# The S1 block of a weight pair added by DMA transfers from the Pool queue, in a one-core hybrid decoder step

## The chip, the cores and the metric

The kernel runs on one core of a Trainium2 chip. The metric is the device time of one execution in microseconds, as the median of several runs. Three runs of the kernel before gave 1041.46, 1042.13 and 1044.23 us.

## The reference, cut to what matters

One decoder layer is computed in float32 for 560 tokens (16 meta + 512 prompt + 32 sample): a SwiGLU feed-forward, a mixer (attention beside a short convolution), and a second SwiGLU feed-forward, each followed by a layer norm. The change touches only the two feed-forwards, and of them only the product with the gate and up weights:

```
D_MODEL = 1024; D_FF = 2816
def swiglu(x, wg, wu, wd):
    return (jax.nn.silu(x @ wg) * (x @ wu)) @ wd
x = layer_norm(DN_ALPHA * x + 0.5 * swiglu(x, wg_l[0], wu_l[0], wd_l[0]), g_l[0], b_l[0])
y, ks, vs, cs = token_mixer(x, attend, conv_prev, w_in_l, conv_w_l, w_out_l)
x = layer_norm(DN_ALPHA * x + y, g_l[1], b_l[1])
x = layer_norm(DN_ALPHA * x + 0.5 * swiglu(x, wg_l[1], wu_l[1], wd_l[1]), g_l[2], b_l[2])
```

## The kernel before, in words

**Units.** TensorE (PE) works through a list of weight units made by `plan_units`. A unit is one buffer of 128 x 1024 weights. Every unit is split in two before PE uses it: ScalarE (ACT) writes the rounded part (`w_hi` or `more_hi`), VectorE (DVE) subtracts it from the source to get the rest (`w_lo` or `more_lo`), and PE multiplies hi by hi, hi by lo and lo by hi. The split of a unit is made while PE works on units some places before it: `following(n)` names the unit that takes over the buffer of unit n, six places on.

**The pair stage.** In each feed-forward f (0 and 1) the first 256 columns of gate and up are done plainly ("gu"). The other 2560 columns are taken in ten pairs j = 0 to 9, each of 256 gate and 256 up columns. A pair is a 2 x 2 block product (blocks: upper and lower half of the contraction, gate and up; two halves of the tokens), done with seven block products instead of eight. Its four weight blocks are loaded by SP: a11 and a12 are the two halves of gate, a21 and a22 the two halves of up. The seven units s = 0 to 6 of a pair use a11, a12, S2, S1, the changed a11, the changed a12, and a22. Four block sums make them, all by DVE in `block_sum`, all 128 x 1024:

- sum 0: a11 <- a11 - a21 (in place)
- sum 1: a21 <- a21 + a22 (in place; this is the block S1, read by unit s = 3)
- sum 2: S2 <- a22 - a11
- sum 3: a12 <- a12 - S2 (in place)

Sum 0 must be over before sum 1, since it reads a21. Pairs 0 to 3 form chunk 0 and are followed by products with the down weights ("dn"); pairs 4 to 9 form chunk 1 and are followed by more of these.

**Order.** Every engine works through its own list in order; semaphores tie them together. While PE is in step s of pair j (`pair_step` of ACT and DVE), the two others do this, j+1 being the next pair:

| step s of pair j | ACT | DVE |
|---|---|---|
| 1 | hi of unit 0 of j+1; silu of the first half | c11 add; lo of unit 0 of j+1 |
| 2 | copy u2; hi of unit 1 | lo of unit 1; sums 0 and 1 |
| 3 | copy p5; hi of unit 2 (S2) | sums 2 and 3; lo of unit 2 |
| 4 | hi of unit 3 (S1) | c22 add; lo of unit 3 |
| 5 | silu of the second half; hi of unit 4; h1 hi | c12 add; lo of unit 4; h1 |
| 6 | h0 hi; hi of unit 5 | h0; lo of unit 5; h1 lo; h0 lo |
| 0 of j+1 | copy p1; hi of unit 6 | lo of unit 6 |

PE waits for copy p1 before step 2 of the same pair, for copy u2 before step 4, for copy p5 before step 5 and for the c22 add before step 6. For the first pair of a feed-forward (j = 0) the order is written out by hand in `gate_up_first`, where sum 1 comes after sum 3. For pair 4 the sums are made while PE is in the down products.

**Names and lines.** L1785 is the block sum, L1793 `block_lo`, L1364 `block_hi`, L1043 PE's pair product, L1442 copy p1, L1448 copy u2, L1452 copy p5, L1462 and L1469 the silus, L1472 and L1465 h1 hi and h0 hi, L1888 the c11 add, L1893 the c22 add, L1897 the c12 add, L714 SP's load of a block. Raw block buffers are called `w_raw` and `more_raw`. Pool (GpSimd) has no instruction in the pair stage.

Of the kernel before, what the change touches and what calls it, by code (L numbers as in the profile page):

```python
# [28 lines left out]
P = 128  # L29
# [33 lines left out]
QT = KT // 2  # L63
# [3 lines left out]
N_PAIRS = FT // 2 - 1  # L67
# [36 lines left out]
def pair_unit(f, j):  # L104
    return UNITS.index(("st", f, j, 0))
# [148 lines left out]
LOADS, RAW, LOAD_BEFORE, ARRIVED = plan_loads()  # L254
# [63 lines left out]
def build(nc, x_prompt, x_sample, cache_k, cache_v, state_conv, meta_tokens, rel_bias, w_in, conv_w,  # L318
# [4 lines left out]
    with ctx:  # L323
# [3 lines left out]
        def sem(name):  # L327
            return ctx.enter_context(nc.semaphore(name))
# [103 lines left out]
        weights_in = [sem(f"weights_in{i}") for i in range(RAWS)]  # L432
# [21 lines left out]
        combo_hi = sem("combo_hi")  # L454
        combo_ready = sem("combo_ready")
        blocks_summed = sem("blocks_summed")
        p1_copied = sem("p1_copied")
        u2_copied = sem("u2_copied")
        p5_copied = sem("p5_copied")
# [85 lines left out]
        def raw(key, k):  # L545

            r = RAW[key]
            return (w_raw[:, r, :] if r < SLOTS else more_raw[:, r - SLOTS, :]).rearrange("p (k n) -> p k n", k=k)

        def split_hi(n, k):  # L550
            at = SLOT[n]
            return (w_hi[:, at, :] if at < SLOTS else more_hi[:, at - SLOTS, :]).rearrange("p (k n) -> p k n", k=k)

        def split_lo(n, k):
            at = SLOT[n]
            return (w_lo[:, at, :] if at < SLOTS else more_lo[:, at - SLOTS, :]).rearrange("p (k n) -> p k n", k=k)

        def split_sum(n):

            at = SLOT[n]  # L560
            return (w_sum[:, at, :] if at < SLOTS else more_sum[:, at - SLOTS, :]).rearrange("p (k n) -> p k n", k=1)
# [781 lines left out]
        def _(act):  # L1343
# [8 lines left out]
            def block_hi(f, j, s):  # L1352

                n0 = pair_unit(f, j)
                n = n0 + s
                src = split_sum(n) if s == 2 else raw((n0, ("11", "12", None, "21", "11", "12", "22")[s]), 1)
                if s in (0, 1, 6):
                    key = (n0, ("11", "12", "22")[s // 1 if s < 2 else 2])
                    act.wait_ge(weights_in[RAW[key]], ARRIVED[key])
                else:  # L1360
                    act.wait_ge(blocks_summed, 4 * (N_PAIRS * f + j) + ({4: 1, 2: 2, 5: 3, 3: 4} if j == 0 else {4: 1, 3: 2, 2: 3, 5: 4})[s])
                if BEFORE[n] is not None:
                    act.wait_ge(steps_done, FREE[BEFORE[n]])
                nc.scalar.activation(split_hi(n, 1), src, ACT.Copy).then_inc(hi_ready, 1)  # L1364
# [357 lines left out]
            for k in range(WO_STEPS):  # L1722
                s = len(WI_STEPS) - AB + k
# [31 lines left out]
        def _(dve):  # L1755
# [9 lines left out]
            def block_sum(f, j, i):  # L1765

                n0, q = pair_unit(f, j), N_PAIRS * f + j
                a11, a12, a21, a22 = [raw((n0, b), 1) for b in ("11", "12", "21", "22")]
                s2 = split_sum(n0 + 2)
                if i == 0:  # L1770
                    dve.wait_ge(weights_in[RAW[n0, "21"]], ARRIVED[n0, "21"])
                    out, a, b, op = a11, a11, a21, ALU.subtract
                elif i == 1:
                    dve.wait_ge(weights_in[RAW[n0, "22"]], ARRIVED[n0, "22"])
                    out, a, b, op = a21, a21, a22, ALU.add
                elif i == 2:
                    dve.wait_ge(blocks_summed, 4 * q + 1)
                    dve.wait_ge(weights_in[RAW[n0, "22"]], ARRIVED[n0, "22"])
                    if BEFORE[n0 + 2] is not None:
                        dve.wait_ge(steps_done, FREE[BEFORE[n0 + 2]])  # L1780
                    out, a, b, op = s2, a22, a11, ALU.subtract
                else:
                    dve.wait_ge(blocks_summed, 4 * q + (2 if j == 0 else 3))
                    out, a, b, op = a12, a12, s2, ALU.subtract
                nc.vector.tensor_tensor(out, a, b, op).then_inc(blocks_summed, 1)  # L1785

# [8 lines left out]
            def next_lo(n):  # L1795

                if n is None:
                    return
                if UNITS[n][0] != "st":
                    weight_lo(n)  # L1800
                    return
                _, f, j, s = UNITS[n]
                if s == 2:
                    block_sum(f, j, 2)
                    block_sum(f, j, 3)
                block_lo(f, j, s)
                if s == 1:
                    block_sum(f, j, 0)
                if s == (2 if j == 0 else 1):
                    block_sum(f, j, 1)  # L1810

            def hidden(f, half, ab, first=False):

# [492 lines left out]
            for k in range(WO_STEPS):  # L2306
                s = len(WI_STEPS) - AB + k
# [39 lines left out]
        @block.gpsimd  # L2347
        def _(pool):
            def weight_lo(n):

                pool.wait_ge(hi_ready, n + 1)
                k = (KT - POOL_TILES) * P
                nc.gpsimd.tensor_tensor(split_lo(n, 1)[:, 0, k:], raw((n, ""), 1)[:, 0, k:],
                                        split_hi(n, 1)[:, 0, k:].bitcast(F32), ALU.subtract).then_inc(lo_pool, 1)

            def ln_sum_squares(L):
                s = ln_sum[:, L % 2, 0:ln_width(L)]
                for c in range(1, 4):
                    pool.wait_ge(squared, KT * L + c + 1)
                    if c >= 2:  # L2360
                        pool.wait_ge(sq_pool, 3 * L + c - 1)
                    nc.gpsimd.tensor_tensor(s, squares_of(L, 0) if c == 1 else s, squares_of(L, c), ALU.add
                                            ).then_inc(sq_pool, 1)

            def convolve(e):
                c, half = CONV_ORDER[e]
                pool.wait_ge(z_dve, step_count("h", c, half))
                if e >= 1:
                    pool.wait_ge(taps_added, 2 * e)
                if c >= 2:  # L2370
                    pool.wait_ge(z_dve, step_count("bg", c - 2, half))
                n = HALF if half == 0 else PROMPT - HALF
                for j in range(3):
                    w = C0 + CT * j + c
                    at = half * HALF + j
                    last = nc.gpsimd.tensor_scalar(taps[:, j, 0:n], u_p[:, c, at:at + n], coef[:, w:w + 1], None, ALU.mult)
                    if half:
                        last = nc.gpsimd.tensor_scalar(
                            taps[:, j, n:HALF].rearrange("p (b t) -> p b t", b=DEC_BATCH),
                            u_s[:, c, :, j:j + DEC_SEQ], coef[:, w:w + 1], None, ALU.mult)  # L2380
                last.then_inc(taps_done, 1)
                pool.wait_ge(taps_done, e + 1)
                nc.gpsimd.tensor_tensor(taps[:, 0, :], taps[:, 0, :], taps[:, 1, :], ALU.add).then_inc(taps_added, 1)
                pool.wait_ge(taps_added, 2 * e + 1)
                nc.gpsimd.tensor_tensor(conv[:, half, c % 2, :], taps[:, 0, :], taps[:, 2, :], ALU.add
                                        ).then_inc(taps_added, 1)

            for n in range(4):
                weight_lo(n)
            for L in range(2):  # L2390
                ln_sum_squares(L)
            for m in range(AB, len(WI_STEPS)):
                u, half = WI_STEPS[m]
                if WI_ORDER[u][0] == "h":
                    if m == WI_STEPS.index((WI_ORDER.index(("h", 0)), 0)):
                        pool.wait_ge(zero_done, 2)
                        pool.wait_ge(kct_copied, 1)
                    convolve(CONV_ORDER.index((WI_ORDER[u][1], half)))
            for k in range(WO_STEPS):
                if k == 8:  # L2400
                    ln_sum_squares(2)
            ln_sum_squares(3)
            pool.wait_ge(norm_rows_in, 32)
            for half in range(2):
                for i, (t, b) in enumerate(y_units(half, True)):

                    w, feats = Y_TILES[t][2], slice(512 * b, 512 * b + 512)
                    y = y_rows[0:w, t, feats]
                    pool.wait_ge(rows_normed, 2 * half + i + 1)
                    nc.gpsimd.tensor_tensor(y, y, g_row[0:w, feats], ALU.mult).then_inc(rows_pool, 1)  # L2410
                    pool.wait_ge(rows_pool, 2 * half + i + 1)
                    nc.gpsimd.tensor_tensor(y, y, b_row[0:w, feats], ALU.add).then_inc(y_pool, 1)
# [23 lines left out]
```

The launch sets the part of each SBUF partition kept for descriptors of Pool's DMAs:

```
nc = bacc.Bacc("TRN2", target_bir_lowering=False, num_devices=1, dynamic_dma_scratch_size=1024)
```

## Time and profile before

| | |
|---|---|
| median of 3 runs | 1042.13 us |
| the profiled execution, whole time | 1044.41 us |
| its span | 1042.6 us |
| mean granted TensorE clock | 0.982 |
| PE busy | 994.1 us (95%) |
| DVE busy | 690.8 us (66%) |
| ACT busy | 467.2 us (45%) |
| POOL busy | 69.6 us (7%) |
| DMA mean | 104 GB/s |

The profile is of one execution. Times in its views are microseconds from the start of the span. "Idle before <- releaser" says how long an engine stood still before an instruction and what released it. [...]

### The profile page before, as it was taken

What the parts mean: (1) busy time and instruction counts of PE and PEld (TensorE: products, weight loads), DVE (VectorE), ACT (ScalarE), POOL (GpSimd) and SP (SyncE); (2) the same over time, 40 slices, a digit from 0 to 9 for tenths busy, and PEclk for the clock granted to TensorE, in tenths of its full rate; (3) what the DMA queues carried; (4) which work ended last, traced back from release to release, by engine and by line L of the source; (5) the groups of instructions that cost most, each with busy time, mean ns of one, the idle gap of its engine ahead of it and who ended that gap; (6) DMA issues with size and microseconds to landing.
All of it is one profiled execution on the core that took longest, in us unless ns stands there. A gap on an engine that the chain in (4) does not pass through costs nothing. (4 is left out here: it accounts for less than half of the span.)

```text
span 1042.6 us, 18161 instructions
## 1 busy us (share of the span) xinstructions
PE 994.1 (95%) x7526; PEld 970.7 (93%) x7526; DVE 690.8 (66%) x990; ACT 467.2 (45%) x780; POOL 69.6 (7%) x80
## 2 busy tenths in 40 slices
PE   8979999999999999999999989679999999999994
PEld 7979999999999999999988988679999999999994
DVE  5887843577886468626666687787743587784457
ACT  4445531245445235545556456444521344553230
POOL 2000000000000000016142000000000000000004
PEclk9989999999999999999999999889999999999998
DMA  9463343133225333452113461033342222336402
GB/s 254 98 119 107 110 133 102 31 90 125 81 82 173 97 116 81 106 182 82 42 42 94 136 209 57 20 110 103 115 119 62 82 81 82 95 103 194 151 1 86
DMA packets 131594, 108.19 MB, mean 104 GB/s; under 512 B 13138, under 2 KB 129590, under 8 KB 131496
## 3 DMA queue, kind: packets, MB, share of 16 engines
q1 hardware_dynamic: 130368, 105.46, 34.1%
q10 hardware_dynamic: 1144, 1.57, 1.3%
q8 instruction: 60, 0.98, 0.4%
q14 instruction: 22, 0.18, 0.1%
HBM read 103.08 MB, written 4.95 MB: 104 GB/s over the span
## 5 line engine op out<-in xcount | busy, mean ns | idle before, releaser
L1056 PE MATMUL banks<-h_hi,w_hi 128*128 128x280 f32 (+1 forms) x480 | 139.1, 290 | 0.0
L1056 PE MATMUL banks<-h_hi,w_lo 128*128 128x280 f32 (+1 forms) x480 | 139.0, 289 | 0.0
L1056 PE MATMUL banks<-h_lo,w_hi 128*128 128x280 f32 (+1 forms) x480 | 138.8, 289 | 0.0
L877 PE MATMUL banks<-x_hi,w_hi 128*128 128x280 f32 (+1 forms) x416 | 126.3, 304 | 3.1 <-DVE x_lo L2127 0.9
L1043 PE MATMUL banks<-x_hi,w_hi 128*128 128x280 f32 (+1 forms) x400 | 118.5, 296 | 9.3 <-ACT ln_sq L1452 7.4
L877 PE MATMUL banks<-x_lo,w_hi 128*128 128x280 f32 (+1 forms) x416 | 120.8, 290 | 0.0
L877 PE MATMUL banks<-x_hi,w_lo 128*128 128x280 f32 (+1 forms) x416 | 120.7, 290 | 0.0
L1043 PE MATMUL banks<-x_hi,w_lo 128*128 128x280 f32 (+1 forms) x400 | 117.5, 294 | 0.0
L1043 PE MATMUL banks<-x_lo,w_hi 128*128 128x280 f32 (+1 forms) x400 | 117.3, 293 | 0.0
L1762 DVE TENSOR_TENSOR w_lo<-w_raw,w_hi 128x1024 fp32r<-128x1024 f32 (+1 forms) x66 | 77.9, 1182 | 56.6 <-ACT w_hi L1350 56.6
L1043 PE MATMUL banks<-t_hi,w_hi 128*128 128x280 f32 x336 | 99.7, 297 | 9.8 <-ACT silu_g L1442 8.8
L1043 PE MATMUL banks<-t_lo,w_hi 128*128 128x280 f32 x336 | 99.4, 296 | 0.0
L1043 PE MATMUL banks<-t_hi,w_lo 128*128 128x280 f32 x336 | 99.3, 295 | 0.0
L1350 ACT ACTIVATE w_hi<-w_raw 128x1024 fp32r<-128x1024 f32 x66 | 68.2, 1039 | 50.2 <-PE banks L1056 27.8
L1056 PEld LDWEIGHTS banks<-h_hi,w_hi 128*128 128x128 f32 x480 | 90.3, 188 | 0.0
L1056 PEld LDWEIGHTS banks<-h_hi,w_lo 128*128 128x128 f32 x480 | 90.3, 188 | 0.0
L1056 PEld LDWEIGHTS banks<-h_lo,w_hi 128*128 128x128 f32 x480 | 90.2, 188 | 0.0
L1043 PEld LDWEIGHTS banks<-x_hi,w_hi 128*128 128x128 f32 x400 | 77.0, 193 | 11.7 <-issue 11.7
L877 PEld LDWEIGHTS banks<-x_hi,w_hi 128*128 128x128 f32 x416 | 78.8, 189 | 7.1 <-DVE x_lo L1978 2.0
L1793 DVE TENSOR_TENSOR w_lo<-w_raw,w_hi 128x1024 fp32r<-128x1024 f32 x38 | 46.5, 1223 | 56.9 <-ACT w_hi L1364 56.9
L877 PEld LDWEIGHTS banks<-x_lo,w_hi 128*128 128x128 f32 x416 | 78.8, 189 | 1.5 <-issue 0.5
L877 PEld LDWEIGHTS banks<-x_hi,w_lo 128*128 128x128 f32 x416 | 78.8, 189 | 0.0
(236 smaller groups left out, 2660.0 us busy)
## 6 DMA issues: line engine op xcount, KB each, us to landing
w_raw<-in_ffn_w_down SPq DMA_DIRECT2D x30, 512.0 KB, 4.0
more_raw<-in_ffn_w_down SPq DMA_DIRECT2D x28, 512.0 KB, 3.6
w_raw<-in_ffn_w_gate SPq DMA_DIRECT2D x24, 512.0 KB, 4.0
w_raw<-in_ffn_w_up SPq DMA_DIRECT2D x24, 512.0 KB, 4.7
more_raw<-in_ffn_w_gate SPq DMA_DIRECT2D x20, 512.0 KB, 4.1
more_raw<-in_ffn_w_up SPq DMA_DIRECT2D x20, 512.0 KB, 5.5
w_raw<-in_w_in SPq DMA_DIRECT2D x14, 512.0 KB, 4.6
w_raw<-in_w_out SPq DMA_DIRECT2D x32, 128.0 KB, 3.0
```

Of the source, the lines that this page charges most:

```text
L877: mm = nc.tensor.matmul(out[:, 0:n], w[:, t, :], x(k), start=(k == ends[0] and w is hi and x is rhs_hi), stop=(k == ends[1] and w is lo))
L1043: mm = nc.tensor.matmul(out[:, ab, c0:HALF], w[:, k, ab * P:(ab + 1) * P], b(t, k), start=(new and k == 0 and w is hi and t[0] is x_hi), s ...
L1056: mm = nc.tensor.matmul(out, w[:, k - k0, c * P:(c + 1) * P], h[:, k, cols(half, f)], start=(k == 0 and w is hi and h is h_hi), stop=(ku = ...
L1350: nc.scalar.activation(split_hi(n, 1)[:, 0, 0:k], raw((n, ""), 1)[:, 0, 0:k], ACT.Copy).then_inc(hi_ready, 1)
L1762: nc.vector.tensor_tensor(split_lo(n, 1)[:, 0, 0:k], raw((n, ""), 1)[:, 0, 0:k], split_hi(n, 1)[:, 0, 0:k].bitcast(F32), ALU.subtract).the ...
L1793: nc.vector.tensor_tensor(split_lo(n, 1), src, split_hi(n, 1).bitcast(F32), ALU.subtract).then_inc(lo_ready, 1)
```

## The change

The block sum 1 (S1) leaves DVE. Pool issues, for each pair, two DMA transfers of 256 KB that read the a22 block again from the weights in HBM and add it into the a21 block in SBUF. Pool waits for sum 0 first. ACT's hi of unit 3 waits for the two transfers by a new semaphore `s1_summed`; the counts of `blocks_summed` go from four to three in a pair. Pool's list gets the ten pairs of feed-forward 0 after its first four weight splits and the ten of feed-forward 1 after the sums of squares of layer-norm half L = 3. The loads of a21 and a22 by SP stay, as do sums 0, 2 and 3.

```diff
@@ block_hi (ACT)
                     act.wait_ge(weights_in[RAW[key]], ARRIVED[key])
+                elif s == 3:
+                    act.wait_ge(s1_summed, 32 * (N_PAIRS * f + j + 1))
                 else:
-                    act.wait_ge(blocks_summed, 4 * (N_PAIRS * f + j) + ({4: 1, 2: 2, 5: 3, 3: 4} if j == 0 else {4: 1, 3: 2, 2: 3, 5: 4})[s])
+                    act.wait_ge(blocks_summed, 3 * (N_PAIRS * f + j) + {4: 1, 2: 2, 5: 3}[s])
@@ block_sum (DVE)
-                elif i == 1:
-                    dve.wait_ge(weights_in[RAW[n0, "22"]], ARRIVED[n0, "22"])
-                    out, a, b, op = a21, a21, a22, ALU.add
                 elif i == 2:
-                    dve.wait_ge(blocks_summed, 4 * q + 1)
+                    dve.wait_ge(blocks_summed, 3 * q + 1)
                 else:
-                    dve.wait_ge(blocks_summed, 4 * q + (2 if j == 0 else 3))
+                    dve.wait_ge(blocks_summed, 3 * q + 2)
@@ next_lo (DVE)
                 if s == 1:
                     block_sum(f, j, 0)
-                if s == (2 if j == 0 else 1):
-                    block_sum(f, j, 1)
@@ Pool
+            def second_row_sum(f, j):
+
+                n0, q = pair_unit(f, j), N_PAIRS * f + j
+                pool.wait_ge(blocks_summed, 3 * q + 1)
+                w = w_up[0, f].rearrange("(k p) n -> p k n", p=P)
+                for k in range(0, QT, 2):
+                    nc.gpsimd.dma_start(raw((n0, "21"), QT)[:, k:k + 2, :],
+                                        w[:, QT + k:QT + k + 2, (2 + 2 * j) * P:(4 + 2 * j) * P],
+                                        accum_op=ALU.add).then_inc(s1_summed, 16)
+
             for n in range(4):
                 weight_lo(n)
+            for j in range(N_PAIRS):
+                second_row_sum(0, j)
@@ Pool, after the loop over WO_STEPS
             ln_sum_squares(3)
+            for j in range(N_PAIRS):
+                second_row_sum(1, j)
```

## Rows read from the trace of the kernel before

**Rows 1.** Part 1 of the page: busy time, share, instructions.

```profile
PE 994.1 (95%) x7526; PEld 970.7 (93%) x7526; DVE 690.8 (66%) x990; ACT 467.2 (45%) x780; POOL 69.6 (7%) x80
```

**Rows 2.** Windows: stretch, busy of each engine, clock, DMA share, GB/s.

```profile
877.00:899.00 22.00, 21.81 (x172) 21.62 (x171) 17.56 (x19) 11.20 (x15) 0.00 (x0) 1.00 0.31 96
61.00:66.00 5.00, 0.50 (x3) 0.50 (x3) 4.45 (x5) 2.14 (x3) 0.00 (x0) 0.79 0.61 105
68.00:70.00 2.00, 2.00 (x10) 2.00 (x10) 1.97 (x3) 0.44 (x1) 0.00 (x0) 0.50 0.73 148
660.00:669.00 9.00, 0.24 (x3) 0.09 (x1) 8.97 (x10) 3.40 (x6) 0.00 (x0) 0.76 0.00 0
681.00:684.00 3.00, 0.14 (x2) 0.00 (x0) 2.48 (x4) 2.11 (x3) 0.00 (x0) 1.00 1.09 372
686.00:688.00 2.00, 2.00 (x11) 2.00 (x9) 2.00 (x2) 0.00 (x0) 0.00 (x0) 0.50 0.00 0
```

**Rows 3.** Waits of PE: line, releaser, us in total, times, longest.

```profile
PE banks L1043 <- DVE ln_sq L1893: 2.5, 14, 0.2
```

**Rows 4.** Timeline of DVE, one pair: start, us, instruction, [idle before <-releaser].

```profile
707.82 2.35 DVE L1785 TENSOR_TENSOR more_raw<-more_raw 128x1024 f32<-128x1024 f32 x2
...
713.62 0.73 DVE L1893 TENSOR_TENSOR ln_sq<-ln_sq,banks 128x560 f32<-128x560 f32 x1
714.26 1.22 DVE L1793 TENSOR_TENSOR w_lo<-more_raw,w_hi 128x1024 fp32r<-128x1024 f32 x1
...
721.97 1.23 DVE L1793 TENSOR_TENSOR more_lo<-more_raw,more_hi 128x1024 fp32r<-128x1024 f32 x1 [1.66 <-ACT more_hi L1364]
...
725.52 0.70 DVE L1888 TENSOR_TENSOR silu_g<-silu_g,banks 128x528 f32<-128x528 f32 x1
...
728.45 1.23 DVE L1793 TENSOR_TENSOR w_lo<-w_raw,w_hi 128x1024 fp32r<-128x1024 f32 x1 [1.09 <-ACT w_hi L1364]
729.59 2.35 DVE L1785 TENSOR_TENSOR w_raw<-w_raw 128x1024 f32<-128x1024 f32 x2
```

**Rows 5.** Timeline of ACT, the same pair.

```profile
712.30 1.04 ACT L1364 ACTIVATE w_hi<-more_raw 128x1024 fp32r<-128x1024 f32 x1
716.16 0.67 ACT L1462 ACTIVATE ln_sum<-ln_sum 128x560 f32<-128x560 f32 x1 [2.82 <-DVE ln_sum L1897]
...
721.84 0.62 ACT L1442 ACTIVATE silu_g<-banks 128x560 f32<-128x560 f32 x1
...
726.25 0.65 ACT L1469 ACTIVATE silu_g<-silu_g 128x528 f32<-128x528 f32 x1 [1.40 <-DVE silu_g L1888]
726.83 0.64 ACT L1448 ACTIVATE ln_sum<-banks 128x560 f32<-128x560 f32 x1
727.37 1.05 ACT L1364 ACTIVATE w_hi<-w_raw 128x1024 fp32r<-128x1024 f32 x1
```

**Rows 6.** Timeline of PE, three places in feed-forward 1.

```profile
668.94 0.57 PE L1043 MATMUL banks<-t_hi,w_hi 128*128 128x280 f32 x1 [8.76 <-ACT silu_g L1442]
...
691.21 0.36 PE L1043 MATMUL banks<-x_hi,more_hi 128*128 128x264 f32 x1 [2.29 <-DVE w_lo L1793]
...
723.53 0.29 PE L1043 MATMUL banks<-t_hi,w_hi 128*128 128x280 f32 x1
```

**Rows 7.** Timelines of DVE and ACT: pair 0 (S1), pair 4 (sum 0, next ACT work).

```profile
663.80 1.22 DVE L1785 TENSOR_TENSOR more_raw<-more_raw 128x1024 f32<-128x1024 f32 x1
...
805.21 1.22 DVE L1785 TENSOR_TENSOR w_raw<-w_raw 128x1024 f32<-128x1024 f32 x1
...
818.01 1.06 ACT L1364 ACTIVATE w_hi<-w_raw 128x1024 fp32r<-128x1024 f32 x1 [4.97 <-PE banks L1056]
```

**Rows 8.** DMA issues: median us from issue to landing; block loads of 650 to 760.

```profile
w_raw<-in_w_in SPq DMA_DIRECT2D x14, 512.0 KB, 4.6
w_raw<-in_w_out SPq DMA_DIRECT2D x16, 256.0 KB, 3.4
w_raw<-in_w_in SPq DMA_DIRECT2D x8, 256.0 KB, 3.9
...
DMA to landing us min/median/max: 3.8/4.3/6.3
```

More of the change, by code:

```diff
@@ L456, in build @@
         blocks_summed = sem("blocks_summed")
+        s1_summed = sem("s1_summed")
         p1_copied = sem("p1_copied")
```

## The prediction

> **What bounds the kernel now.** I read part 1 of the page first: TensorE is busy 95% of the span, DVE 66%, Pool 7% [rows 1]. So a microsecond taken from DVE counts only where PE waits for it. The windows say where that is. In the middle of the pair stage PE is busy 21.81 of 22 us with DVE at 17.56 [rows 2]. PE stands still in two places, the entry into the pair stage of each feed-forward: 4.5 of 5 us from 61 to 66, 8.8 of 9 us from 660 to 669, and nearly all of 681 to 684, with DVE busy through most of each. PE's own waits end on ACT's copy p1 (8.76 us, at 668.94) and on a DVE weight split (2.29 us, at 691.21) [rows 6]; inside the stage the c22 add costs 14 waits of at most 0.2 us, 2.5 us in all [rows 3].
>
> The timelines of one pair say more than the busy shares. DVE and ACT form a closed loop of hand-overs with next to no slack. From lo of unit 3 (714.26) to the next sum 0 (729.59) every stop of one engine is ended by the other, and none by PE: DVE c12 add, ACT silu (waited 2.82 us for DVE), hi and lo of unit 4, h1, h1 hi, h0 hi, hi of unit 5, lo of unit 5 (waited 1.66 for ACT), h1 lo, h0 lo, lo of unit 6, c11 add (725.52), silu, copy u2 (726.83), hi of unit 1, lo of unit 1 (waited 1.09), sum 0 [rows 4, 5]. That is 729.59 - 714.26 = 15.33 us of a period of 729.59 - 707.82 = 21.77 us. The rest is the DVE queue: sums 0 to 3, lo of unit 2, c22 add, lo of unit 3. DVE's average of 80% in this stage hides that the loop is as long as PE's own work.
>
> **Part 1: what the removal gives.** 20 sums leave DVE. Two in a row take 2.35 us and one alone 1.22 [rows 4, 7], so each holds the queue for 1.13 us, 22.6 us in all. It lies beside PE work except where the loop or the heads end a wait of PE: (a) pair 0, where S1 at 663.80 stands in the chain that ends in copy p1: 1.13 us in each feed-forward [rows 6, 7]; (b) the c22 add of the next pair, before PE's step 6 at 691.21: another 1.13 us each; (c) the 2.5 us of waits for the c22 add [rows 3]. Sum, if nothing replaces it: 4 x 1.13 + 2.5 = 7 us. No more, because PE's work is then the next bound.
>
> **Part 2: what the new wait adds.** The wait stands in ACT's in-order list before hi of unit 3. Behind it on ACT stand the silu of the second half, hi of unit 4, h1 hi, h0 hi, hi of unit 5 and copy p1; on DVE, lo of unit 3 waits for that hi, and the c12 add and everything after it stand behind lo. So the transfer enters the loop. Let L be the time from the end of sum 0 to the start of hi of unit 3 by way of Pool's wait, two issues, the landing and the semaphore. Nothing else is in Pool's queue there (busy 0.00 in the stage [rows 2]), and SP's queue is not passed.
>
> - From hi to lo: 728.45 - 727.37 = 1.08 us [rows 4, 5], then 15.33 us, then 1.18 us of sum 0 (half of the pair's 2.35). New loop: 17.59 + L. Old period: 21.77. Each further pair costs L - 4.18.
> - PE notices at step 2, by copy p1. It ended at 721.84 + 0.62 = 722.46, 8.20 us after lo of unit 3, so 9.28 us after hi starts. PE's step 2 began at 723.53, which is 14.53 us after sum 0's end (709.00) [rows 4 to 6]. The first late block of a chunk costs PE L - 5.25.
> - Chunk 1 has five such blocks (pairs 5 to 9): 4(L - 4.18) + (L - 5.25) = 5L - 21.97. Chunk 0 has three (pairs 1 to 3) and begins 1.13 us early by (a): 3L - 14.74. Both feed-forwards: 16L - 73.4.
> - Pairs 0 and 4 are covered. Sum 0 of pair 4 is over at 806.4 and ACT's next work stands at 818.01 [rows 7]; less 2 us for hi and its queue, L up to 9.6 is free there. In pair 0 it is about 8 us.
>
> **What L is.** No row has a Pool DMA or an adding one. The nearest: a 256 KB block of SP lands 3.4 to 3.9 us after its issue, a 512 KB block 4.6 in the median, and the loads of this stage 3.8 to 6.3 [rows 8]. From below: both transfers fly as one plain load would, L = 3.8, where the change gains. From above: two in a row, each as long as the slowest load, 12.6. I take two in a row, since the code cuts the block in two where SP's loads are whole: 2 x 3.65, plus 2 x 0.6 for reading the destination as well (the step from 256 to 512 KB, 4.6 - 3.9 = 0.7, nearly). That is 8.5 with no charge for Pool's own work in making the transfers, for which there is no row. HBM is no limit: 20 x 512 KB more beside 93 to 96 GB/s.
>
> [...]
>
> With L = 8.5: 16 x 8.5 - 73.4 = 63 us.
>
> **The clock.** A PE that stood 2.9 us (681 to 684) runs at 0.50 from 686 to 688; one that stood 4.5 us is at 0.50 from 68 to 70 [rows 2]. These spells last some 3.3 and 5 us and cost half of that, 1.6 and 2.5. Here PE would stop 4.3 us in each pair: I take 2.0. In the loop copy u2 waits for PE's step 2: without PE it would come 12.57 + 1.08 = 13.65 us after hi of unit 3, and step 2 now ends 9.4 + 3.1 + 2.0 = 14.5 us after it. So 0.9 us in each of 12 pairs, and 2.0 in full in the last pair of each of 4 chunks: 11 + 8 = 19 us.
>
> **Sum.** 63 + 19 = 82 us on the profiled execution's 1044.4, which is 1126. That execution is 2.3 us above the median of the runs: on the median 1124. I say 1125.
>
> **Rivals.**
> - A, the other side: the transfers land within 4.2 us, so the loop gets shorter and the 7 us of part 1 come through: 1037 on the profiled execution, 1035 on the median. It decides at L = 4.18, and at 73.4 / 16 = 4.6 the account is even. For it: a plain 512 KB block lands in 3.8 at best [rows 8]. Against: Pool has to be woken, there are two transfers, and each also reads its destination. Chance 0.07. [...]
> - B, overlap: the second is issued while the first moves. L = 5.5 to 7, 16L - 73.4 = 15 to 39, clock up to 10: 1060 to 1091. Chance 0.22.
> - C, Pool starved: making the transfers is slow, or slowed by DVE's block sums that run just then (sums 2 and 3, lo, c22 add, 4.6 us without a gap [rows 4]). L = 12 to 13, 119 to 135 us and a clock loss of 35: about 1200. [...] Chance 0.13.
> - D: L about 4.6, no change. Chance 0.03.
>
> **The numbers.** Forecast 0.55 (L from 7 to 11). The range goes from L = 5.6 (16 us, no clock loss: 1060) to L = 11.5 (111 us and 27 of clock: 1182). A measurement of this kernel tells 0.3%, 3 us, from no change. Slower 0.90, same 0.03, faster 0.07.
>
> **What would show it.** In the profile after: ACT's wait before hi of unit 3, ended by a DMA, 16 times, and L read from it; sum 0 to sum 0 spaced by 17.6 + L, some 26 to 27 us; PE idle at step 2 (first instruction with t_hi, released by copy p1, L1442) about 4 us in each pair, with the clock at 0.50 behind it; the wait for the c22 add gone. The stages outside the pairs keep their times. It is wrong if the spacing stays at 21.7, if PE's new stops stand elsewhere, or if L is not constant over the pairs.

## The result, and the profile after

The change makes the kernel slower: a median of 1156.88 us (4 runs, 1154.89 to 1158.46) beside 1042.07 for the kernel before on the same chip. The ratio is 1.110, 95% interval 1.108 to 1.112. The forecast was 1125 with a range of 1060 to 1182, and slower. The profiled execution took 1158.46 us with a span of 1156.7, which is 114.1 more than before; the sum had 82. The mean granted clock (1.00 is full speed) fell from 0.982 to 0.939.

Lines of the changed kernel: copy p1 is L1445, `block_hi` L1367, PE's pair product L1044, the c22 add L1891, the block sum L1785 and `block_lo` L1793 as before, Pool's transfer L2392. Part 1 of its page:

```profile
PE 1024.2 (89%) x7526; PEld 1001.1 (87%) x7526; DVE 670.3 (58%) x970; ACT 467.7 (40%) x780; POOL 118.5 (10%) x120
```

DVE has 20 instructions and 20.5 us less than in [rows 1], as reckoned (22.6). PE has as many matmuls as before and is busy 30.1 us longer with them: they run longer where the clock is at half (behind the stop shown below, at 0.50, one starts every 0.23 us, and at 1.00 every 0.13 us). The waits of PE in the changed kernel (line, releaser, us in total, times, longest):

```profile
PE banks L1044 <- ACT h_f L1445: 59.6, 10, 14.1
PE banks L1044 <- ACT silu_g L1445: 38.9, 7, 8.3
PE banks L1044 <- ACT ln_sq L1455: 7.6, 2, 4.5
```

Seventeen waits end on copy p1, 98.5 us in all: the 16 pairs, 5.6 us each in the mean (the prediction had about 4; without the one of 14.1 us it is 5.1), and one entry, whose 8.3 us stand against the 8.76 of [rows 6]. The c22 add of [rows 3] is gone from the list. In ACT's own list of waits, 20 stand before a hi (L1367) and end on the new transfers:

```profile
ACT w_hi L1367 <- DMA w_raw<-in_ffn_w_up: 54.8, 6, 16.2
ACT w_hi L1367 <- DMA more_raw<-in_ffn_w_up: 46.7, 8, 7.6
ACT more_hi L1367 <- DMA w_raw<-in_ffn_w_up: 27.4, 4, 7.6
ACT more_hi L1367 <- DMA more_raw<-in_ffn_w_up: 16.3, 2, 8.5
```

One pair shows how the time is passed on. DVE's sum 0 ends about 776.3, and the next one stands 28.21 us behind this one, where [rows 4] have 21.77:

```profile
775.11 1.22 DVE L1785 TENSOR_TENSOR more_raw<-more_raw 128x1024 f32<-128x1024 f32 x1
...
787.02 1.23 DVE L1793 TENSOR_TENSOR w_lo<-more_raw,w_hi 128x1024 fp32r<-128x1024 f32 x1 [6.39 <-ACT w_hi L1367]
...
803.32 1.22 DVE L1785 TENSOR_TENSOR w_raw<-w_raw 128x1024 f32<-128x1024 f32 x1
```

Pool, the same pair. The second transfer is not issued when the first is made (777.98), but 3.47 us later:

```profile
776.77 1.21 POOL L2392 DMA_DIRECT2D more_raw<-in_ffn_w_up  x1 [23.00 <-DVE more_raw L1785]
781.46 1.22 POOL L2392 DMA_DIRECT2D more_raw<-in_ffn_w_up  x1 [3.47 <-issue]
```

ACT, the same pair: hi of unit 3, and copy p1 behind it.

```profile
785.92 1.06 ACT L1367 ACTIVATE w_hi<-more_raw 128x1024 fp32r<-128x1024 f32 x1 [7.24 <-DMA more_raw<-in_ffn_w_up]
...
794.60 0.62 ACT L1445 ACTIVATE silu_g<-banks 128x560 f32<-128x560 f32 x1
```

PE, and the windows around its stop (columns as in [rows 2]): step 2 starts when p1 is there, and then at half clock, where [rows 6] show step 2 at 723.53 without a stop.

```profile
795.37 0.57 PE L1044 MATMUL banks<-t_hi,w_hi 128*128 128x280 f32 x1 [4.77 <-ACT silu_g L1445]
```

```profile
790.00:795.00 5.00, 0.59 (x5) 0.38 (x4) 2.76 (x4) 3.05 (x5) 0.00 (x0) 0.76 0.31 105
795.00:800.00 5.00, 4.63 (x22) 4.67 (x23) 5.00 (x6) 2.76 (x4) 0.00 (x0) 0.56 0.55 171
800.00:805.00 5.00, 5.00 (x41) 5.00 (x40) 2.90 (x4) 2.22 (x3) 0.10 (x1) 1.00 0.27 91
```

From these rows L is 785.92 - (775.11 + 1.18) = 9.63 us: 0.48 until Pool starts, 4.69 from the first issue to the second, 4.46 from the second issue to hi. The trace has the first transfer landed 4.4 us after its issue began, so the second issue follows that landing by 0.3 us. The 1.21 us in which Pool makes a transfer lie inside these times, as they count from the start of the issue. Read the same way in all 16 pairs that count (not pairs 0 and 4), it is 9.60 to 10.14 in thirteen, and 10.93, 11.35 and 18.55 in three of feed-forward 0. The sum of the 16 is 168.3. The prediction's account then gives 168.3 - 73.4 = 94.9 us, and 19.2 of the 114.1 are left for the clock, for which it had 19.

### The profile page after: what moved, and what is told of

Its sections match the earlier page's. It is cut to its first block and busy times, and to the rows that moved or that the text cites. A ratio compares the mean times of both kernels' runs of the same rounds, so it can differ in the third digit from the quotient of the medians.

```text
span 1156.7 us, 18181 instructions
## 1 busy us (share of the span) xinstructions
PE 1024.2 (89%) x7526; PEld 1001.1 (87%) x7526; DVE 670.3 (58%) x970; ACT 467.7 (40%) x780; POOL 118.5 (10%) x120
## 3 DMA queue, kind: packets, MB, share of 16 engines
q0 software_dynamic: 10880, 10.49, 6.7%
## 5 line engine op out<-in xcount | busy, mean ns | idle before, releaser
L1044 PE MATMUL banks<-t_hi,w_hi 128*128 128x280 f32 x336 | 113.3, 337 | 89.1 <-ACT h_f L1445 50.2
L1044 PEld LDWEIGHTS banks<-t_hi,w_hi 128*128 128x128 f32 x336 | 76.7, 228 | 92.1 <-issue 92.0
L1044 PE MATMUL banks<-x_hi,w_hi 128*128 128x280 f32 (+1 forms) x400 | 118.2, 296 | 8.0 <-ACT ln_sq L1455 7.6
L1044 PE MATMUL banks<-x_hi,w_lo 128*128 128x280 f32 (+1 forms) x400 | 117.8, 295 | 0.0
L1044 PE MATMUL banks<-x_lo,w_hi 128*128 128x280 f32 (+1 forms) x400 | 117.7, 294 | 0.0
L1044 PE MATMUL banks<-t_lo,w_hi 128*128 128x280 f32 x336 | 110.9, 330 | 0.0
L1044 PE MATMUL banks<-t_hi,w_lo 128*128 128x280 f32 x336 | 110.2, 328 | 0.0
L1793 DVE TENSOR_TENSOR w_lo<-w_raw,w_hi 128x1024 fp32r<-128x1024 f32 x38 | 46.5, 1224 | 100.5 <-ACT w_hi L1367 100.5
L1793 DVE TENSOR_TENSOR w_lo<-more_raw,w_hi 128x1024 fp32r<-128x1024 f32 x38 | 46.5, 1224 | 71.9 <-ACT w_hi L1367 71.9
L1044 PEld LDWEIGHTS banks<-x_hi,w_hi 128*128 128x128 f32 x400 | 77.3, 193 | 8.8 <-issue 8.8
```

Of the source, the lines that this page charges most:

```text
L1044: mm = nc.tensor.matmul(out[:, ab, c0:HALF], w[:, k, ab * P:(ab + 1) * P], b(t, k), start=(new and k == 0 and w is hi and t[0] is x_hi), s ...
L1793: nc.vector.tensor_tensor(split_lo(n, 1), src, split_hi(n, 1).bitcast(F32), ALU.subtract).then_inc(lo_ready, 1)
```

## The experiments

Each is measured against the kernel before on its chip. "Account" is the sum of L over the 16 pairs less 73.4; "span" is the difference of the profiled spans to 1042.6. The edits are shown in part ("..." marks what is left out) and, but for the kernel before with the new order, against the changed kernel.

**The wait taken away.** Pool's transfers are left out, so that nobody adds a22 into a21, and hi of unit 3 waits for sum 0 and for a22:

```
-  act.wait_ge(s1_summed, 32 * (N_PAIRS * f + j + 1))
+  act.wait_ge(blocks_summed, 3 * (N_PAIRS * f + j) + 1)
+  act.wait_ge(weights_in[RAW[n0, "22"]], ARRIVED[n0, "22"])
```

> Sum 1 is left out: nobody adds a22 into a21, hi of unit 3 waits only for sum 0 and for the load of a22. My theory (the loop of ACT and DVE lists; the removal is worth 7 us, the rest of the loss is the landing time L in the loop): 1035 us, PE's waits for the c22 add gone, the two entries 2.3 us shorter each, pair period 21.5 us. Rival (the loss, or part of it, comes from the changed order of counts or from DVE's list without sum 1 and not from the transfers): 1042 or above.

Measured: 1031.97 us, ratio 0.989 (0.987 to 0.992). All of the loss goes with the transfers and the wait for them; which of the two it is, the moved reader below tells. The removal by itself is worth 11 us, not 7. A window one period long, and PE's entry into the pair stage of feed-forward 1:

```profile
844.92:866.25 21.33, 21.33 (x170) 21.33 (x169) 16.25 (x19) 11.33 (x14) 0.00 (x0) 1.00 0.33 99
```

```profile
663.08 0.57 PE L1044 MATMUL banks<-t_hi,w_hi 128*128 128x280 f32 x1 [7.62 <-ACT silu_g L1446]
```

The entries give what the prediction said: 7.62 instead of 8.76 and 1.27 instead of 2.29 [rows 6]. But the period fell from 21.77 to 21.33 (in feed-forward 0 from 22.05 to 21.65). Over 16 pairs that would be 6 to 7 us, where the waits for the c22 add, 0.2 us each, summed to 2.5 [rows 3].

**Is adding the price?** The same transfers, copying:

```
-                                        accum_op=ALU.add).then_inc(s1_summed, 16)
+                                        ).then_inc(s1_summed, 16)
```

> The two Pool transfers copy a22 over a21 instead of adding: the addition is left out, everything else as in the change. [...] Rival (Pool always lets one transfer land before it makes the next): gap of 3 us or more stays, L about 9, 1140 us or more.

Measured: 1067.28 us, 1.023 (1.021 to 1.026). Pool makes a pair of copies in one go (x2), and hi follows the issue by 4.2 us:

```profile
852.07 1.45 POOL L2392 DMA_DIRECT2D more_raw<-in_ffn_w_up  x2 [26.84 <-DVE more_raw L1785]
```

```profile
856.26 1.06 ACT L1367 ACTIVATE w_hi<-more_raw 128x1024 fp32r<-128x1024 f32 x1 [2.33 <-DMA more_raw<-in_ffn_w_up]
```

L is 4.3 to 5.2 in these pairs, but 6.4 in pair 9 of feed-forward 0, where the second copy landed late (5.1 us). In 7 of 20, every third, the second copy was made after a wait of 2.7 to 2.8 us, once the first had landed, and L was 6.9 to 7.1 in those that count. One of the seven, pair 1 of feed-forward 0, stands apart with a wait of 10.7 and L = 16.4; its L is long in the two runs that follow too (15.3 and 15.4). Account 23.7, span 24.1. The time is below the author's estimate for this run, 1080 to 1090, which had both copies in flight at once, L at 6.8 (16 x 6.8 - 73 = 35 us) and a clock loss of up to 10.

**Is Pool's wait a matter of space?** The theory of descriptor places has it that the second transfer waits because its descriptors don't fit beside those of the first, and that a larger space takes the wait away. Only the part of SBUF for them is larger, 1408 bytes in each partition in place of 1024:

```
-  dynamic_dma_scratch_size=1024
+  dynamic_dma_scratch_size=1408
```

> [...] Theory of descriptor places: the second issue follows the first without the 3.6 us between, both are in flight, L about 7.5 to 8 us, 16 x 7.8 - 73 = 51 us and some 12 of clock: 1100 to 1110 us. Rival (Pool always waits for a transfer to land, or waits because both add): L stays at 9.7, 1157 us.

Measured: 1106.99 us, 1.062 (1.059 to 1.064). In 16 of 20 pairs both adding transfers are now made without a gap, and L is 6.8 to 7.4; in the other four the second waited as before and L is 9.5 to 9.8.

```profile
772.53 2.47 POOL L2392 DMA_DIRECT2D w_raw<-in_ffn_w_up  x2 [22.84 <-DVE w_raw L1785]
```

```profile
779.44 1.06 ACT L1367 ACTIVATE more_hi<-w_raw 128x1024 fp32r<-128x1024 f32 x1 [4.96 <-DMA w_raw<-in_ffn_w_up]
```

Account 58.9, span 61.9. Nothing but the space was changed, so the wait of the second transfer was for descriptor space, and it is worth 52 of the 114 us, its share of the half clock included. Why four pairs still wait was not found out.

**One transfer instead of two**, 512 KB, with the larger space:

```
-  for k in range(0, QT, 2):   ... [:, k:k + 2, :]
+  for k in range(0, QT, 4):   ... [:, k:k + 4, :]
```

> The change with 1408 bytes for descriptors and one adding transfer of 512 KB in a pair in place of two of 256 KB. Theory: the fixed part of a transfer is paid once. Issue to landing 4.5 us for 256 KB, of which about 2.1 us is data: 6.6 us for 512 KB, plus 0.4 to start, L about 7.2 us, 16 x 7.2 - 73 = 42 us and 10 of clock: 1090 to 1100 us. Rival (making descriptors or moving the data is what costs, not the number of transfers): L 9 or more, 1140 us or more.

Measured: 1084.52 us, 1.040 (1.037 to 1.042). L is 6.3 to 6.8 (7.8 in one pair), and no pair waits for space:

```profile
760.36 1.30 POOL L2392 DMA_DIRECT2D w_raw<-in_ffn_w_up  x1 [22.92 <-DVE w_raw L1785]
```

```profile
766.58 1.06 ACT L1367 ACTIVATE more_hi<-w_raw 128x1024 fp32r<-128x1024 f32 x1 [4.22 <-DMA w_raw<-in_ffn_w_up]
```

Account 41.3, span 41.5. It costs 1.30 us to make one transfer of 512 KB and 1.21 to make one of 256, so the halving had nearly doubled Pool's work. The 512 KB landed 6.0 and 6.2 us after the issue (medians of the two kinds of buffer), where 6.6 was expected and 256 KB took 4.5 and 4.6 in the changed kernel. The time is below the 1090 to 1100 expected: the 10 us of clock in it did not come.

**The transfer kept, its reader moved.** hi of unit 3 moves on ACT from step 4 to behind h1 hi in step 5; lo of unit 3 moves on DVE from step 4 to behind h0 in step 6. PE's order is not touched; the counts of units 3 and 4 change places.

```
+  late = s in (4, 5) and ... swapped(following(n - s + 4))
+  if not (late and s == 4):
       next_hi(following(n))
   ...                        # after h1 hi, in step 5
+  if late:
+      next_hi(following(n - 1))
```

> The change with the same two adding transfers and the same descriptor space, but in every pair except 0 and 4 hi of unit 3 moves in ACT's list behind h1 hi (a step later), and lo of unit 3 in DVE's list behind h0; the counts of the splits are swapped with unit 4. Nothing that PE needs soon stands behind the wait now: the place in ACT's list comes some 10.5 us after sum 0, the transfers take 9.7. Theory of the loop: the loss of 115 us is gone but for pair 1 of the first feed-forward, where L was 18.5 (about 8 us); with the 11 us that leaving out sum 1 gave: 1034 to 1044 us. Rival (Pool's transfers cost by themselves: 10 MB more traffic, DVE or the weight loads slowed): 1060 us or more.

> The kernel before with only the order of the lists changed as in e5: sum 1 stays on DVE at its place. It tells what the order gives by itself. Theory: DVE still has the sum, the c22 add still stands behind four sums, so 1040 to 1044 us; the difference to e5 is then what taking the sum off DVE gives. Rival: the order alone is worth the whole 8 to 11 us (1032), or it costs (1050), because lo of unit 3 now sits before PE's use of it.

Measured: the change with this order 1043.32 us, 1.001 (1.000 to 1.002); the kernel before with this order 1043.06 us, 1.001 (1.000 to 1.002). The order alone is worth nothing, and with it the same transfers cost nothing inside the stage but in one pair. So the loss was in the place of the wait and not in the traffic. The transfers themselves are not quicker (4.77 us from issue to issue, 3.56 of it waiting), but the hi that needs them comes later than they land. DVE's sum 0 in this kernel, at pair 1 of feed-forward 0 and in chunk 1 of feed-forward 1:

```profile
63.40 1.22 DVE L1799 TENSOR_TENSOR w_raw<-w_raw 128x1024 f32<-128x1024 f32 x1
94.51 1.22 DVE L1799 TENSOR_TENSOR more_raw<-more_raw 128x1024 f32<-128x1024 f32 x1
...
854.91 1.22 DVE L1799 TENSOR_TENSOR w_raw<-w_raw 128x1024 f32<-128x1024 f32 x1
876.26 1.22 DVE L1799 TENSOR_TENSOR more_raw<-more_raw 128x1024 f32<-128x1024 f32 x1
```

The period is 21.35 us, that of the kernel without any S1 work. What eats the gain seems to be one pair: 31.11 us, its L again 18.6.

**The one late pair left to DVE.** As before, and sum 1 of pair 1 in feed-forward 0 is made by DVE behind sum 0, under its own semaphore; Pool skips it.

```
+  if (f, j) == (0, 1):
+      ...
+      nc.vector.tensor_tensor(a21, a21, a22, ALU.add).then_inc(s1_dve, 1)
```

> e5, but in pair 1 of the first feed-forward sum 1 goes back to DVE (behind sum 0) and Pool leaves that pair out. In e5 the distance from that pair's sum 0 to the next one was 31.1 us against 21.0 in e1, everything else alike. Theory (the late landing of that one pair is all that e5 lost against e1): 1043 - 10 + 1 for the sum that is back: 1032 to 1036 us, faster than both kernels. Rival (the profiled spacing is one case and e5 loses its 11 us in other places too, for instance by the traffic): 1039 or above.

Measured: 1033.48 us (4 runs, 1033.15 to 1034.29), 0.991 (0.990 to 0.993): faster than both kernels, and 9.8 us faster than with that pair on Pool. The same place in its trace, 23.55 us for that pair, which is 7.6 of the 9.8:

```profile
63.21 1.22 DVE L1804 TENSOR_TENSOR w_raw<-w_raw 128x1024 f32<-128x1024 f32 x1
64.35 1.22 DVE L1832 TENSOR_TENSOR w_raw<-w_raw 128x1024 f32<-128x1024 f32 x1
...
86.76 1.22 DVE L1804 TENSOR_TENSOR more_raw<-more_raw 128x1024 f32<-128x1024 f32 x1
```

**Why is that pair late?** In the changed kernel its transfers were issued at 66.52 and, after 12.29 us of waiting, at 80.01, and hi waited 16.16 us:

```profile
66.52 1.20 POOL L2392 DMA_DIRECT2D w_raw<-in_ffn_w_up  x1 [23.72 <-DVE w_raw L1785]
80.01 1.22 POOL L2392 DMA_DIRECT2D w_raw<-in_ffn_w_up  x1 [12.29 <-issue]
```

The DMA queues between 40 and 80 (packets, MB, share), q0 being Pool's, q1 SP's and q10 ACT's:

```profile
q10 hardware_dynamic: 1000, 1.51, 32.3%
q1 hardware_dynamic: 1913, 1.90, 15.9%
q0 software_dynamic: 678, 0.65, 11.9%
```

q10 carries one transfer, ACT's write of the 1472.5 KB table `bias_dram`, issued at 42.74. The kernel before shows its effect on SP's loads already, in a stretch that the prediction did not look at (issues between 50 and 80, KB, median us to landing), where its block loads of 650 to 760 took 4.3 [rows 8]:

```profile
more_raw<-in_ffn_w_gate SPq DMA_DIRECT2D x2, 512.0 KB, 18.3
```

The write, moved behind step 6 of pair 1, where it is issued at 111.56:

```
+  if (f, j, s) == (0, 1, 6):
+      act.wait_ge(table_ready, 1)
+      act.dma_start(bias_dram, bias_row[:, :].unsqueeze(1).to_broadcast(...)).then_inc(bias_out, 16)
```

> The change with one thing moved: ACT's write of the bias table to HBM (1472 KB in small packets, issued at 42.7 us) is issued after pair 1 of the first feed-forward, some 50 us later. Theory (that write, and not the loads of SP, filled the DMA queues when pair 1's transfers flew, L 18.5): L of pair 1 falls to about 9.8, L of pair 2 or 3 rises to 12 or more instead, ACT may wait for the write at pair 3; total 1145 to 1160 us. Rival (the weight loads of SP did it): L of pair 1 stays above 14 us.

Measured: 1163.19 us, 1.115 (1.113 to 1.117), 3 us above the range expected. The late landing goes with the write: L of pair 1 is 10.0, and that of pair 3 is 26.0. Three loads of SP issued just behind the write land in 26 to 30 us.

```profile
75.47 1.06 ACT L1367 ACTIVATE w_hi<-w_raw 128x1024 fp32r<-128x1024 f32 x1 [7.63 <-DMA w_raw<-in_ffn_w_up]
...
148.57 1.06 ACT L1367 ACTIVATE more_hi<-w_raw 128x1024 fp32r<-128x1024 f32 x1 [23.58 <-DMA w_raw<-in_ffn_w_up]
```

Account 102.2, span 120.5.

**Pool's adder instead of the DMA**, in the old order and in the late order:

```
-  for k in range(0, QT, 2):
-      nc.gpsimd.dma_start(..., accum_op=ALU.add).then_inc(s1_summed, 16)
+  nc.gpsimd.tensor_tensor(a21, a21, a22, ALU.add).then_inc(s1_summed, 1)
```

> Sum 1 as one add instruction of Pool on SBUF (a21 <- a21 + a22) in the old order, hi of unit 3 waits for it; no transfer. Pool's adds of 128x384 took 1.13 to 1.65 us in the trace of before, so 128x1024 takes 3.0 to 4.4 and L is 3.1 to 4.6. Theory (only L matters, 4.2 to 4.6 is the break-even): 1032 to 1045 us. Rival (Pool and DVE get in each other's way, both reading two SBUF operands): DVE's sums 2 and 3 or Pool's add get longer, L 6 or more, 1065 us or more.

> e7 with the lists of e5: Pool's add, and hi of unit 3 a step later. Theory: the add is covered like the transfers, without their traffic and without the late one in pair 1: 1032 to 1036 us, the whole of what leaving out sum 1 gave (1032). Rival (Pool's add slows DVE's own sums beside it): the c22 add comes later than PE wants it, 1040 us or more.

Measured: 1063.28 us, 1.020 (1.019 to 1.022), and 1063.66 us, 1.021 (1.020 to 1.023). In both the rival came true. L is 3.6 us in the first of the two, which by the account would be a gain. The reordering that hid the transfer hides nothing here, because what is lost is lost on DVE: the c22 add comes late, and PE's waits for it are 17.5 us where they were 2.5 [rows 3]. PE, Pool and DVE in the first of the two:

```profile
PE banks L1044 <- DVE ln_sq L1891: 17.5, 14, 1.3
```

```profile
869.76 3.45 POOL L2392 TENSOR_TENSOR w_raw<-w_raw 128x1024 f32<-128x1024 f32 x1 [19.41 <-DVE w_raw L1785]
```

```profile
869.72 1.23 DVE L1785 TENSOR_TENSOR w_sum<-w_raw 128x1024 f32<-128x1024 f32 x1
870.98 3.32 DVE L1785 TENSOR_TENSOR w_raw<-w_raw,w_sum 128x1024 f32<-128x1024 f32 x1
```

DVE's sum 3 takes 3.32 us instead of 1.22 and ends 1.1 us after Pool's add (873.21), as if it had begun only then; DVE's sum 2, begun 0.04 us before Pool's add, takes its usual 1.23. The period grows to 22.85 us. What begins second is the longer one, DVE's sum 3 by 2.1 us, and Pool's add too: it takes 3.40 to 3.45 us behind a DVE sum that began first, but 2.39 and 2.40 in the two pairs 4, where no DVE sum is running when it begins. Pool's making of a transfer shows nothing of the kind: it took 1.20 to 1.22 us with DVE's sums right beside it, and they took 1.22.

## Why the prediction was right, and where its sizes were off

- **The mechanism held.** The wait stands in ACT's list and from there enters the loop of ACT and DVE; PE notices at step 2 by copy p1; the spacing is 17.59 + L plus about a microsecond (28.21 - 17.59 - 9.63 = 0.99; over the twelve spacings 0.4 to 1.8, forecast 0.9). In pairs 0 and 4, with L = 9.7 to 10.0, PE has no new stop, though the prediction had only 8 us free in pair 0. Between the two feed-forwards the time stays: two stops of PE stand 213.97 us apart before and 213.62 after. Leaving out the transfers and the wait turned +114 us of the span into -12, and moving the reader behind the landing turned it into -2.
- **The account 16L - 73.4 held where most pairs have L of 4.3 to 7.4.** It is off by 0.4 us for the copies, 0.2 for the one transfer and 3.0 for the larger space. Only where PE's stops are 4 us and more is there a rest: 19.2 for the change and 18.3 with the moved table write. PE's busy time is 1024.2 and 1023.4 us in these, and 999.1, 1001.8 and 1005.6 in the three others.
- **The clock term fits, to a tenth only by luck**: 19 us forecast, 19.2 left over. The excess over 17.59 + L sums to 14.9 us in the twelve spacings, where the forecast had 11. Against it stand 3.2 us, as the old spacings were longer than the 21.77 that the account takes for all of them (22.05 in feed-forward 0). Outside the spacings 7.5 are left, where it had 8. That this rest is all clock is argued from the windows and PE's busy time; no run took the clock alone away.
- **L was mis-sized**: 8.5 taken, 168.3 / 16 = 10.5 measured, 32 us of the time. The step that failed is "2 x 3.65, plus 2 x 0.6 with no charge for Pool's own work". "Two in a row" was right, and HBM was no limit, as taken: while the two transfers of the pair shown above flew, the DMA moved 52 GB/s (776 to 781) and 51 (781 to 786.5), where [rows 2] have 372 in one window. One adding transfer of 256 KB landed 4.4 to 4.7 us after its issue in most pairs, near the 4.25 taken, with Pool's making of it (1.21 us) inside. What the sum left out is the start of Pool (0.48) and the 0.3 us between a landing and the next issue; together this makes 9.6 to 10.1. The rest is "L constant over the pairs", which the prediction itself named as a sign of being wrong: pair 1 of feed-forward 0 has 18.55, because of the table write, and two others about 11, because a first transfer landed in 5.6 to 5.9 us, for which no cause was looked for. Pair 1 alone is 8.7 us of the 32.
- **Part 1 was undersized**, 7 us taken and 11 measured: the term for the waits on the c22 add. The stops that PE shows there (0.2 us) were not all that was lost; the period shows 0.4, and no run says where the other 0.2 went.
- **The second transfer waits for descriptor space.** With 1024 bytes in each partition the second adding transfer waited in 20 of 20 pairs, with 1408 bytes in 4. How many places an adding transfer takes was not measured; that a second plain copy waited in only 7 of 20 pairs, and a second adding transfer in all of them, says that it is more than a copy takes.
- **The rivals.** A and D fall with L at 9.6 and more. B (overlap, L 5.5 to 7) did not happen here, but is what the larger space brought: 61.9 us against its 15 to 49, since L there was 7.1 in the median, 9.5 to 9.8 in four pairs and 15.3 in one. C falls with its L of 12 to 13, and with its reason: Pool was held by space, not by slow making (1.21 us) nor by DVE.

## What to carry to other kernels

Before a wait is added, write down what stands behind it in that engine's list and whether the list is part of a loop. If it is, all of the latency beyond the loop's slack (4.2 us here) counts in every turn, however idle the engine that causes it. A transfer of 10 us costs nothing where its reader stands far enough behind its issue, so move the reader first, and look for the one place where other traffic stretches the transfer: here it ate nearly the whole gain. Read the worth of a removed instruction from the period of the loop, not from the waits of the bottleneck engine.

## What the runs showed of the hardware

- An adding transfer of 256 KB issued by Pool took 1.21 us to make and landed 4.5 us after its issue, the making included; a plain copy took 0.72 us to make and landed after 3.1 to 3.3 us in most pairs. Where two were in flight, L was 7.1 (adding, larger space) against 4.6 (copies) in the median, and the queue shows smaller packets for the same 10.49 MB: in the changed kernel 10880, in the one with plain copies 3200.

```profile
q0 software_dynamic: 10880, 10.49, 6.7%
```

```profile
q0 software_dynamic: 3200, 10.49, 3.3%
```

- One write to HBM (1472.5 KB, ACT's queue) stretched the landing of a 256 KB transfer of Pool from 4.7 us, in the run with the write moved, to 13.1 us. SP's 512 KB loads of the same place went from 4.0 and 4.8 us in the median (gate and up) to 20.4 and 18.6. Of the DMA engines' time 60% was taken (32.3, 15.9 and 11.9% in the rows above).
- Pool's add of two 128 x 1024 blocks took 2.4 us where no DVE sum was running when it began, and 3.40 to 3.45 beside DVE's sums, of which one took 3.32 in place of 1.22.
